# Expert weights of a two-block transformer: pieces of two experts with 8 KB per row, used in pairs, for pieces of four experts with 4 KB

## The reference, cut to what matters

```
def expert_choice_moe(h, w_router, w_gate, w_up, w_down):   # 16 experts, cap = 32 tokens each
    aff = softmax(einsum('bnd,de->bne', h, w_router))
    g, idx = top_k(swapaxes(aff, 1, 2), cap)
    xs = h[idx]                                             # (16, 32, 1024)
    hid = silu(einsum('becd,edf->becf', xs, w_gate)) * einsum('becd,edf->becf', xs, w_up)
    y = einsum('becf,efd->becd', hid, w_down) * g[..., None]
    return zeros(n, d).at[idx].add(y)
```

## Time and profile before

| | us |
|---|---|
| median of 3 runs (lowest, highest) | 1672.36 (1672.15, 1678.78) |
| span of the profiled execution | 1675.7 |
| MoE of layer 0, first gather to last down | 1076.3 to 1306.4 |
| MoE of layer 1, first gather to the end | 1465.1 to 1675.7 |

### The profile page before, as it was taken

The page is one execution under the profiler, slowest core; times in us unless marked ns, Lnnn a source line. Parts: engine busy times, 40 slices in busy tenths (PEclk is TensorE's granted clock), DMA queues, the critical chain, the costliest instruction groups (busy, mean ns, idle before and its releaser), DMA issues.

```text
span 1675.7 us, 22597 instructions
## 1 busy us (share of the span) xinstructions
PE 1557.6 (93%) x9541; PEld 1123.0 (67%) x9541; DVE 695.0 (41%) x1635; ACT 347.3 (21%) x811; POOL 96.6 (6%) x113
## 2 busy tenths in 40 slices
PE   6998999999999999999999999999999999996656
PEld 3785788888776788888887878744544776842212
DVE  2334377777416378877433134402212334310011
ACT  3144310000114330010124243310010334211100
POOL 0003200000002310000011102000000002000000
PEclk8999999999999999999999999899999999998988
DMA  9568579996583268669363244499999444789997
GB/s 354 175 232 284 207 278 352 344 341 244 195 241 124 86 219 310 233 247 335 127 226 111 73 151 178 175 403 409 409 409 397 174 151 168 283 349 409 409 409 306
DMA packets 167705, 441.02 MB, mean 263 GB/s; under 512 B 7690, under 2 KB 19636, under 8 KB 167604
## 3 DMA queue, kind: packets, MB, share of 16 engines
q1 hardware_dynamic: 166800, 439.12, 70.4%
q10 hardware_dynamic: 804, 0.45, 0.1%
HBM read 438.51 MB, written 1.05 MB: 262 GB/s over the span
## 4 chain that ended last, share of the span: by engine, by line
PE 77%; DMA 11%; issue 3%; ACT 3%; POOL 2%; PEld 1%; DVE 1%; SPq 1%; ACTq 0%; PEldq 0%; DVEq 0%
PE bank L688 74%; DMA ring<-in_w_down 4%; DMA scr<-in_w_gate 3%; DMA ring<-in_w_up 3%; PE bank L699 2%; POOL scr L2424 2%; PEld bank L688 1%; DMA ring<-in_l_mod_w 1%; SPq L621 1%; PE bank L744 1%; ACT scr L2027 0%; ACTq L2189 0%; ACT hT L1965 0%; ACT brow L1982 0%; DVE scr L2491 0%
## 5 line engine op out<-in xcount | busy, mean ns | idle before, releaser
L688 PE MATMUL bank<-hT,ring 128*128 128x256 f32 (+1 forms) x2416 | 477.8, 383 | 4.9 <-ACT hT L1965 3.8
L688 PEld LDWEIGHTS bank<-hT,ring 128*128 128x128 f32 (+1 forms) x2416 | 384.3, 177 | 83.5 <-issue 11.9
L688 PE MATMUL bank<-scr,ring 128*128 128x256 f32 (+3 forms) x1764 | 378.4, 377 | 2.0 <-DVE mods L2590 1.1
L688 PEld LDWEIGHTS bank<-scr,ring 128*128 128x128 f32 (+2 forms) x1764 | 311.9, 186 | 54.9 <-issue 9.8
L2572 DVE SCALAR_TENSOR_TENSOR scr<-scr,csil 128x512 f32<-128x512 f32 x420 | 293.6, 752 | 3.2
L688 PE MATMUL bank<-scr 128*32 128x512 f32 (+8 forms) x1504 | 202.6, 427 | 15.7 <-ACT scr L2392 3.8
L688 PE MATMUL bank<-ring,scr 128*32 128x512 f32 (+2 forms) x1408 | 179.7, 588 | 19.9 <-DMA ring<-in_w_down 13.6
L688 PEld LDWEIGHTS bank<-scr 128*32 128x32 f32 (+4 forms) x1504 | 123.8, 153 | 89.3 <-issue 74.0
L688 PEld LDWEIGHTS bank<-ring,scr 128*32 128x32 f32 (+2 forms) x1408 | 68.2, 118 | 121.0 <-issue 87.7
L2424 POOL TENSOR_SCALAR scr<-scr,small 128x256 f32<-128x256 f32 (+2 forms) x88 | 79.8, 926 | 1009.5 <-DVE small L2627 855.1
L1993 ACT ACTIVATE scr<-bank 128x256 f32<-128x256 f32 x44 | 16.9, 384 | 376.8 <-PE bank L688 376.8
(11 more groups left out here) (307 smaller groups left out, 1085.6 us busy)
## 6 DMA issues: line engine op xcount, KB each, us to landing
ring<-in_w_down SPq DMA_DIRECT2D x25, 2048.0 KB, 23.8
scr<-in_w_ada SPq DMA_DIRECT2D x23, 2048.0 KB, 9.5
ring<-in_w_gate SPq DMA_DIRECT2D x23, 2048.0 KB, 15.5
scr<-in_w_up SPq DMA_DIRECT2D x19, 2048.0 KB, 22.7
scr<-in_l_mod_w SPq DMA_DIRECT2D x14, 2048.0 KB, 15.7
ring<-in_w_up SPq DMA_DIRECT2D x13, 2048.0 KB, 16.4
ring<-in_l_mod_w SPq DMA_DIRECT2D x10, 2048.0 KB, 12.0
ring<-in_l_ffn_wg SPq DMA_DIRECT2D x10, 2048.0 KB, 13.6
```

The lines of the kernel that those rows point to most:

```text
L688: ins = nc.tensor.matmul(out, lhsT, rhs, start=start, stop=stop, skip_group_check=True)
```

## The change

The pieces of gate, up and down stay 2 MB and stay in the same slots and order, but each now holds two experts, and 8 KB in one stretch per partition and expert: for gate and up four neighbouring rows (512h+4p to 512h+4p+3), for down two (256h+2p and 256h+2p+1). Two pieces, a pair, make up the half h of a matrix for all four experts. PE waits for both at the start of a pair, walks over k (4 chunks for gate and up, 2 for down) and in each over the four experts, and releases the first piece in the last chunk after expert 1, the second after expert 3. The last group's down pieces keep their old cuts: whole rows of 4 KB for two, half rows of 2 KB for two.

The order of features follows: `gather` reads `xtok` with every fourth column (16 bytes from element to element), the transposes of the hidden values read every second column, and `shift_and_pairs` has 16 small matmuls of 32 columns for 8 of 64, for which DVE first copies eight columns of shifts into `acol`.

```
         def moe_source(layer, kind, group, s):
             w = A[("w_gate_2", "w_up_2", "w_down_2")[kind]][layer]
+            half, pair = s // 2, s % 2
             if kind < 2:
-                return w.rearrange("(g e) (s p two) n -> g s p e (two n)", e=GE, p=P, two=2)[group, s]
+                return w.rearrange("(g q e) (h p k) n -> g h q p e (k n)", q=2, e=2, h=2, k=4)[group, half, pair]
             if in_halves(layer, group):
                 if s >= 2:
-                    return w.rearrange("(g e) (f s p) (q n) -> g s q p (e f) n", e=GE, s=2, p=P, q=2)[group, 1, s - 2]
-                s *= 2
-            return w.rearrange("(g e) (s p) n -> g s p e n", e=GE, p=P)[group, s]
+                    return w.rearrange("(g e) (h p k) (q n) -> g k q p (e h) n", e=GE, h=2, k=2, q=2)[group, 1, s - 2]
+                return w.rearrange("(g e) (h p k) n -> g h k p e n", e=GE, h=2, k=2)[group, s, 0]
+            return w.rearrange("(g q e) (h p k) n -> g h q p e (k n)", q=2, e=2, h=2, k=2)[group, half, pair]
...
-                for two in range(2):
-                    for hi in range(2):
-                        o = MODO[3] + (3 * 8 + hi) * 2
-                        for kind, cols in enumerate((acol[:, 64 + hi:64 + hi + 7:2], mods[:, o:o + 13:4])):
-                            mm(b[hi * HD:(hi + 1) * HD, NE + 8 * two + 4 * kind:NE + 8 * two + 4 * kind + 4],
-                               ident[:, two:P:2], cols, start=False, stop=True,
-                               signal=pe_to_dve if two and hi and kind else None)
+                for k in range(4):
+                    for q in range(4):
+                        mm(b[32 * q:32 * q + 32, NE + 4 * k:NE + 4 * k + 4], ident[:, k:P:4],
+                           acol[:, 56 + q:56 + q + 13:4], start=False, stop=True,
+                           signal=pe_to_dve if k == 3 and q == 3 else None)
...
-                                cols = slice(256 * (2 * half + c // 2) + c % 2, 256 * (2 * half + c // 2 + 1), 2)
+                                cols = slice(512 * half + c, 512 * (half + 1), 4)
...
-                        for s4 in range(4):
-                            if layer and kind == 0 and s4 == 2:
+                        for half in range(2):
+                            if layer and kind == 0 and half:
                                 pe.wait_ge(xs_ready, n["xs"])
-                            w = use(("moe", layer, kind, g, s4)).rearrange("p (e s n) -> p e s n", e=GE, s=2)
-                            for c2 in range(2):
-                                c = 2 * s4 + c2
+                            w = [use(("moe", layer, kind, g, 2 * half + pair)).rearrange(
+                                "p (e k n) -> p e k n", e=2, k=4) for pair in range(2)]
+                            for k in range(4):
+                                c = 4 * half + k
                                 for i, s in enumerate(streams):
                                     for j in range(GE):
-                                        last = c2 == 1 and i == ns - 1 and j == GE - 1
+                                        last = k == 3 and i == ns - 1 and j % 2
                                         mm(banks[2 * s + kind][32 * j:32 * j + 32, :],
-                                           xs[s][:, c, 32 * j:32 * j + 32], w[:, j, c2, :], start=(c == 0),
-                                           stop=(c == DC - 1), signal=slots_released if last else None)
+                                           xs[s][:, c, 32 * j:32 * j + 32], w[j // 2][:, j % 2, k, :],
+                                           start=(c == 0), stop=(c == DC - 1),
+                                           signal=slots_released if last else None)
...
-                            turn(banks[2 * s][:, f * P:(f + 1) * P], hid[s][:, f * P:(f + 1) * P],
+                            cols = slice(256 * (f // 2) + f % 2, 256 * (f // 2 + 1), 2)
+                            turn(banks[2 * s][:, f * P:(f + 1) * P], hid[s][:, cols],
                                  hid_turned if f == 3 else None)
...
                     for f in range(4):
-                        w = use(("moe", layer, 2, g, f)).rearrange("p (e n) -> p e n", e=GE)
+                        if f % 2 == 0:
+                            w = [use(("moe", layer, 2, g, f + pair)).rearrange(
+                                "p (e k n) -> p e k n", e=2, k=2) for pair in range(2)]
...
             def mixers_last():
                 norm_root(std)
                 norm_scale(cT, hc, hc, std, lambda c: ac(5, c))
+                nc.vector.tensor_copy(ac(7, 0, 8), mod(3, 3, 0, 8))
                 link(scale_cols(8, 3, 4))
```

More of the change, by code:

```diff
@@ L1808, in experts @@
                                 for j in range(GE):
-                                    last = half == 1 and i == ns - 1 and j == GE - 1
+                                    last = f % 2 and half == 1 and i == ns - 1 and j % 2
                                     mm(banks[4 + 2 * s + half][32 * j:32 * j + 32, :],
                                        hidT[s][:, f, 32 * j:32 * j + 32],
-                                       w[:, j, half * 512:(half + 1) * 512], start=(f == 0), stop=(f == 3),
-                                       signal=slots_released if last else None)
+                                       w[j // 2][:, j % 2, f % 2, half * 512:(half + 1) * 512], start=(f == 0),
+                                       stop=(f == 3), signal=slots_released if last else None)
                     pe.drain().then_inc(y_ready, 1)
@@ L2366, in take_gathered @@
                             for c in range(4):
-                                at = 8 * (c % 2) + 2 * half + c // 2
+                                at = 4 * c + half
                                 ins = nc.scalar.activation(xs[s][:, 4 * half + c, :], b[:, c * P:(c + 1) * P],
-                                                           ACT.Identity, scale=pair_cols[:, at:at + 1],
-                                                           bias=pair_cols[:, at + 4:at + 5])
+                                                           ACT.Identity, scale=pair_cols[:, at + 2:at + 3],
+                                                           bias=pair_cols[:, at:at + 1])
                             ins.then_inc(xs_ready, 1)
```

## The result

The changed kernel takes 1705.24 us, the median of 4 runs (1705.06 to 1705.67), for 1675.57 us of the kernel before on the same chip (4 runs, 1672.15 to 1678.82). The ratio is 1.017, with a 95% interval of 1.0153 to 1.0186: slower by 1.7%. The forecast of 1672.7 us and its range, 1665 to 1702, both missed it; the mechanism that came is that of rival 1. The forecast stood on three runs of the kernel before with a median of 1672.36 us; a fourth, at 1678.82, has moved that median up by 3.2 us.

The account below looks back on a forecast made before the run. PE was taken to bound layer 0 and weight transfers layer 1; -4.2 (transfers) + 1.3 (restart) + 0.65 (small matmuls) + 2.3 + 0.3 (strides) = +0.3 us, giving 1672.7 us, range 1665 to 1702.

Parts of the forecast that it names:

- rival 1: Gathers, mainly layer 0: stride-four stationary loads run at half rate, costing 30.2 us for 2.3; 1700.6 us; chance 0.35.
- The step that failed: Gathers of layer 0 and layer 1's first: every fourth column costs 8 ns more on each of 288 records, 2.3 us.
- The transposes of hidden values: 32 in layer 0, 4 at layer 1's end: going from no stride to two costs 8 ns each, 0.3 us.
- Transfers of layer 1: Layer 1's MoE: 8 KB rows cut a piece from 5.117 to 4.99 us; 33 pieces save 4.2 us.
- Rivals 2 and 3: Layer 1 transfers: longer rows gain 9.2 us, chance 0.08; or 8 KB rows travel as two packets, saving nothing, 0.07.
- Rival 2: Layer 1 transfers: 4.84 us per piece at 430 GB/s, strides free, 9.2 us saved; 1665.1 us; chance 0.08.
- The restart: Start of layer 1's MoE: pairs release the first slot after 14 matmuls, not 8; queue starts 1.3 us later, all on path.
- Layer 0's cover: Layer 0's MoE: last down piece keeps 3.4 us to spare, so PE does not wait; costed at nothing.
- The small matmuls: shift_and_pairs: 16 records more at 0.04 us each cost 0.65 us on PE, on the path.
- DVE's copy: Copy of eight columns beside PE's projections, about 0.16 us; costed at nothing, at most 0.2.

Follow-up runs that it names:

- sorted copies: Changed kernel, but ACT's copies making xtok sort the features, so gathers read without a step: 1674.49 us, ratio 0.997 to the kernel before.

## Why the prediction was wrong

**The step that failed.** "The nearest rows are those of stride two: I take the same 8 ns again, 2.3 us." It cost 236 - 121 = 115 ns a record, and 115 x 288 = 33.1 us. Layer 0 alone: 256 x 0.115 = 29.4 of the 29.9 found there. I had carried on the 8 ns of step two as if the price were one per step. But 64 lines are where a second limit begins to bind (1.84 x 64 = 118 ns and 121 measured, against 114 without a step), and from there the time grows with every line. A small difference right at such a crossing says nothing of the slope behind it. The row of DVE at 64-byte steps was weighed against the load being slow; ACT's free 16-byte steps confirm that row, and it still told nothing of PE. The transposes of hidden values, whose step is the cheap two, had 0.3 us set for them, and that was right: PE's rows for eight of them in layer 0 read 1.11 us for 1.04 three times and 1.34 for 1.25 once, 0.3 us in all, and the last row of four in layer 1 reads 0.75 for 0.66.

**Rival 1** had the right mechanism and nearly the size: 105 ns and 30.2 us for 115 and 33.1. It had a chance of 0.35 only, though it rested on a stated rule that changed the sum by 28 us, against which stood one row of another engine. Its price was set a little low, at twice the 113 ns of a record without a step. The range ended at 1702 and the time was 1705: 2.9 us too little are in that price, and 3.2 are the median of the kernel before, 1675.57 for 1672.36. By the ratio the change costs 28.4 us on the forecast's base, and rival 1 had 28.2. That its sum came out so near is in part luck: the clock between the two MoE (-1.6), the small matmuls (-0.6) and the transfers (-0.9 by the tail) made up for the 2.9.

**Transfers of layer 1: right.** Pairs 9.97 us apart were promised (its own 4.99 a piece makes 9.98). PE's timeline after (start us, us, instruction):

```profile
1583.00 5.98 PE L689 MATMUL bank<-ring,ctxT 128*32 128x512 f32 x32 [6.37 <-DMA ring<-in_w_gate]
...
1672.73 1.07 PE L689 MATMUL bank<-scr,ctxT 128*32 128x512 f32 x2 [6.32 <-DMA ring<-in_w_up]
```

Nine pairs in 89.73 us are 9.97 each. Over 28 pieces the stretch of 139.57 us gives 4.985 each, so 33 x (5.117 - 4.985) = 4.4 us for the 4.2 forecast, at 421 GB/s for 419. The kernel with 8 KB rows and nothing else had 5.1 us in its tail (210.6 - 205.5). Rivals 2 and 3 are out by the same rows. Rival 2's 4.84 us a piece would need about 432 GB/s (409 x 5.117 / 4.84), not the 430 written, which changes nothing.

**The restart: right in kind, a little small.** SP's issue came 1504.33 - 1500.66 = 3.67 us behind the start of gate for the 3.4 forecast and 1.98 before: 1.7 later for 1.3. Why 1.7 for six matmuls, which the sum had at 1.3, no run shows. Two runs price the pairs by the tail: 207.1 with them and 205.5 without is 1.6, SP's issue coming 3.67 us behind gate in the one and 1.99 in the other; undoing the pairs at the start brought 1.3.

**Layer 0's cover: right in the kernels where it can be read.** No row of PE in layer 0's MoE waits for a transfer. After the change that proves little, since PE is 30 us slower; but with the step of two put back, first gather to first spread behind the last down is 231.9 us for 231.6.

**The small matmuls: wrong, 0.02 us for 0.65.** Sixteen of 32 columns take as long as eight of 64:

```profile
1434.26 0.66 PE L689 MATMUL bank<-acol,tab 128*32 128x4 f32 x32
```

From their start to the next row are 1.15 us for 1.13. I had multiplied the count and kept the pace: the matmuls came 21 ns apart by the record for 42. That four tiles of 32 columns ran beside each other where two of 64 did is my reading; no run varies it.

**What wasn't in the sum:** -1.7 us between the two MoE. Rows of stretches at the same eight products behind those small matmuls, before and after:

```profile
1405.90:1410.50 4.60, 4.60 (x8) 1.47 (x8) 2.22 (x11) 1.74 (x4) 4.47 (x3) 0.63 0.80 286
```

```profile
1435.40:1440.00 4.60, 4.59 (x18) 2.29 (x19) 3.69 (x17) 2.67 (x6) 4.46 (x3) 1.00 0.79 262
```

The granted clock was 0.63 in the one execution and 1.00 in the other. It accounts for 1.6 us (the eight records took 4.68 us for 3.04). It is no work of the change: the kernel with only the step of four took 4.68 us there and the unchanged order with a step of three 3.04. Nothing is left in this stretch for DVE's copy, costed at nothing. **The tail's sum** then is +3.7 (32 records at 115 ns) + 1.7 - 4.4 = +1.0 for the +0.3 found. With the 5.1 us that 8 KB rows brought by themselves in place of the 4.4 it is +0.3: the tail gained a little more than the cadence over 28 pieces says, and what the difference of 0.7 is stays open.

## What to carry to other kernels

Before a layout is chosen for longer rows of a transfer, count the 16-byte lines that the stationary operand of every load will then touch: in float32 a step of two is nearly free here, and a step of four nearly doubles the time of a gather whose products have 128 columns (236 ns a record for 121). If the order of features must change, try letting the engine that copies out of a bank do the sorting: here it cost ACT nothing. A cost that is small at one size is carried on only when it is known which limit it comes from; where the trace has one point and a stated rule puts a threshold between it and the new one, the rule deserves more weight than a line through that point had here.

## What the runs showed of the hardware that was not expected

- Loads with 128 lines weren't slowed by a lower clock. After the change the first stream's half of the first gather took 7.73 us at a granted clock of 0.79, the second stream's 7.63 at 1.00, and layer 1's first two gathers 7.73 each at 0.78 and 1.00. A gather without a step took 5.47 us at 0.68 (sorted copies) and 3.84 at 1.00 (the run without a step); with 96 lines, the step of three, it was 6.46 us at 0.73 and 5.86 at 1.00. The rows are those after the change:

```profile
1075.89:1083.60 7.71, 7.71 (x33) 7.71 (x34) 0.90 (x4) 0.59 (x1) 0.00 (x0) 0.79 0.00 1
...
1083.45:1091.08 7.63, 7.63 (x33) 7.44 (x32) 0.00 (x0) 1.17 (x2) 0.00 (x0) 1.00 0.00 0
```

- Rows of a transfer stay whole packets up to 16 KB, and the rate still rises there, 421 to 426 GB/s, though less than from 4 to 8 KB.
- Sixteen matmuls on tiles of 32 columns took the time of eight on tiles of 64, 0.66 us.
